# Moving bulk copies between DMA queues, and four orders of work, in a hybrid decoder-layer kernel

## The chip, the cores and the metric

The kernel runs on one NeuronCore of one Trainium2 chip. The metric is the device time of one execution in microseconds (us), the median over several runs. TensorE is written PE, its weight loads PEld, VectorE is DVE, ScalarE is ACT, GpSimd is POOL, SyncE is SP. SP does no arithmetic here: it issues DMA transfers. ACT and POOL issue some too.

## What is computed

One decoder layer for a prompt of 512 tokens and for 8 sample sequences of 4 new tokens each (32 tokens), with shared weights of width 1024. Cut to what matters:

```python
proj = h @ w_in                                   # q, k, v, z, xBC, dt
att  = dilated attention over k, v (16 heads; the samples also over 2048 cached rows)
xbc  = silu(causal_dwconv(xBC)); dt = softplus(dt + bias)
y    = ssd_scan(xs, dt, A, B, C, D)               # chunks of 128 tokens
ssm  = gated_rmsnorm(y, z, ssm_norm_g)
h1   = layer_norm(ALPHA * h + concat(att, ssm) @ w_out)
q    = h1 @ w_q; top 16 + top 16 keys -> 16 of 16384 experts for each of 8 heads
out  = layer_norm(ALPHA * h1 + sum_k gate * gelu(h1 . u[e]) * v[e])
new_k_sample, new_v_sample = caches shifted by 4 rows, with the 4 new rows at the end
```

The last line is bulk traffic: two caches of 8 x 2048 x 1024 floats are copied from HBM to HBM, less four rows each.

## The kernel before, in words

The five engines run one program each (lines 2367 to 2424 list the stages) and meet at semaphores. The stages, in order:

**Projection.** `sp_project` (L292) loads the transposed tokens `xraw` in two halves, chunks 0 to 3 and chunks 4 to 7 of the width, with the small dt weights between them, then streams 44 blocks of `w_in` through a ring of four slots. A product is made in three passes: ACT casts an operand to a high part (L318 for the tokens, L326 for weights), DVE (tokens, L377) or POOL (weights, L363) subtracts to get the low part, and PE multiplies high by high, high by low and low by high (`product`, L186 to L190). The first product is the dt projection, whose chunk c waits for the tokens' low part and for dt's low part, made after chunk 3 (L380). ACT also issues part of the cache copies here: `copy_cache` (L272, issue L277) moves 4088 KB, `copy_half` (L279, issue L283) 2044 KB. `copy_half(eng, y)` for y from 0 to 31 is all of the second cache.

**Attention.** A loop of 67 rounds n, over 64 units (16 heads x 4 tiles of 128 queries), written out by hand. In round n PE makes the scores of unit n (L666), turns the probabilities of unit n - 2 (L673) and multiplies those of unit n - 3 with the values (L682). DVE adds the bias (L785), finds the maximum (L788) and scales (L795); ACT takes the exponential (L860) and copies the turned tile out of the bank (L868). The eight sample sequences b are laid over it: sequence b begins at round 2 + 7b and `at` counts rounds from there (`sample_steps`, L587). At `at` 0 and 1 PE makes its scores from a ring of keys, at 5 and 6 it turns the probabilities, which ACT keeps (L884, L886, L887), at 7 and 9 it multiplies with a ring of four blocks of cached values (L732): blocks 0 to 3 at `at` 7, blocks 4 to 6 at `at` 9. SP loads the block four ahead into a slot as soon as its block is used (`values_of`, L610). At `at` 10 DVE copies the result (L828), at `at` 11 PE turns it (`dec_turn_out`, L736, matmul L741), as the first thing after the round's scores and before `turn(n - 2)`. After its last load SP issues the copies y = 15 to 18.

**SSD.** PE turns and sums five tiles ("fronts", L1064 to L1078), then runs four chunks of 128 tokens and the sample tile. A chunk is `state` (L1118), four `intra` (L1106), four `seg` (L1089 to L1092, two of them for the next chunk) and `inter` (L1130). At the end of chunk i, for i from 1, PE turns the normed chunk i - 1 (`turn_out`, L1031, transpose L1035), which DVE makes late in chunk i (`normed`, L1314, statement L1323); ACT copies it to `mixT` (`keep_out`, L1160, copy L1161). DVE's whole part begins with a wait for the norm vector `normg` (L1245). SP loads it at the start of the stage (L984), then two states, then issues six `copy_cache` and one `copy_half`; after the last chunk's state it stores that and streams `w_out`, with four more `copy_half` (y = 11 to 14) between its first blocks (`sp_out`, L1430). The event orders at L935 to L950 hold each engine's order; each wait asks for a count in such an order.

**Output projection.** 16 chunks of `mixT` by 16 blocks of `w_out` in a ring of eight (L1480), for tiles 0 and 1, then 2, then 3; then the first layer norm.

**Query.** 16 blocks of `peer_wq` by the tokens. SP loads blocks into four raw slots, and issues y = 19 to 31 of the second cache between them (`sp_query`, L1619). ACT, for block f, waits for the query product of f, keeps it (L1707), and casts the raw block f + 4 as soon as it has landed (`hi_of`, L1630, cast L1633). POOL makes the low part (L1640) and so frees the raw slot. PE makes the product of f + 1, then the scores of f (L1689), which need what ACT kept.

**Up and value stages.** 128 blocks of `peer_u` and then 128 of `peer_v` in the same three-pass way, with the choice of experts, the gathers and the gates on DVE and POOL beside them, then the second layer norm. The change touches nothing here.

## Time and profile before

| what | us |
|---|---|
| median of 3 runs | 2127.38 |
| the runs | 2119.74, 2127.38, 2133.82 |
| the profiled execution | 2123.87 |
| its span, first to last instruction | 2122.0 |
| PE busy | 2027.4 (96%) |
| DVE busy | 1488.1 (70%) |
| ACT busy | 743.7 (35%) |
| POOL busy | 784.4 (37%) |
| DMA moved | 683.04 MB |

All stage times below are us from the start of that span. A busy PE is not a PE at full rate, since ends of matmuls are modelled and the clock can be granted at half; so the granted clock is read with it. "Idle before, and what ended it" is inferred from semaphores. The stages lie at: projection 0 to 291, attention 291 to 518, SSD to 640, output projection to 794, query to about 926, up stage to 1560, value stage to 2084.

### The profile page before, as it was taken

To read this page: it belongs to the slowest core of one execution; us is meant where nothing else is said; L and a number is where in the kernel's file an instruction comes from. 1 tells how busy PE (TensorE), PEld (TensorE's weight loads), DVE (VectorE), ACT (ScalarE), POOL (GpSimd) and SP (SyncE) were. 2 spreads that over 40 slices of the span, in tenths; PEclk is the share of its full clock that TensorE was granted. 3 is DMA by queue.
4 is the path that set the end of the run, shared out by engine and by line. 5 is a ranking of instruction groups with operands and counts; after the bars stand their busy time and mean duration, and the time that the engine had idled before them with its cause. 6 is when DMAs were issued, how large, how long until landed. Compare 5 with 4: busy or idle time off the path is not lost.

```text
span 2122.0 us, 33482 instructions
## 1 busy us (share of the span) xinstructions
PE 2027.4 (96%) x12142; PEld 1687.3 (80%) x12142; DVE 1488.1 (70%) x3108; ACT 743.7 (35%) x1112; POOL 784.4 (37%) x483
## 2 busy tenths in 40 slices
PE   7999999997989999899999999999989999999998
PEld 7999965554553339899999999999978887777776
DVE  1276135553672335579889699999689898888988
ACT  3232124443440012134343355655333333333332
POOL 4333310000210003248899732122456555555530
PEclk9999999998989999999999999999999999999999
DMA  8999988788998479738999888878999999999993
GB/s 320 343 331 321 314 316 336 307 324 280 321 335 309 163 290 334 288 123 291 353 354 359 285 308 305 305 277 297 395 384 390 392 392 390 390 383 388 382 363 138
DMA packets 202350, 683.04 MB, mean 322 GB/s; under 512 B 18304, under 2 KB 84224, under 8 KB 194176
## 3 DMA queue, kind: packets, MB, share of 16 engines
q1 hardware_dynamic: 150256, 442.42, 58.0%
q0 software_dynamic: 46080, 167.79, 20.7%
q10 hardware_dynamic: 5904, 71.39, 9.8%
q8 instruction: 65, 1.06, 0.2%
q14 instruction: 45, 0.37, 0.0%
HBM read 618.78 MB, written 196.32 MB: 384 GB/s over the span
## 4 chain that ended last, share of the span: by engine, by line
PE 51%; DMA 24%; issue 11%; DVE 7%; POOL 4%; ACT 2%; SPq 0%; POOLq 0%; DVEq 0%; ACTq 0%
DMA overlay<-peer_v 17%; PE bank L188 10%; PE bank L189 9%; PE bank L190 9%; PE bank L1480 5%; PE bank L2082 4%; POOL overlay L363 4%; DVE overlay L2294 2%; PE bank L682 2%; DMA overlay<-peer_wq 2%; PE bank L666 2%; DMA arena<-w_out 1%; DMA overlay<-peer_u 1%; DVE arena L2095 1%; PE bank L732 1%
## 5 line engine op out<-in xcount | busy, mean ns | idle before, releaser
L188 PE MATMUL bank<-overlay 128*128 128x384 f32 (+4 forms) x2768 | 941.5, 340 | 40.3 <-DVE overlay L2300 21.1
L189 PE MATMUL bank<-overlay 128*128 128x384 f32 (+4 forms) x2768 | 926.5, 335 | 0.0
L190 PE MATMUL bank<-overlay 128*128 128x384 f32 (+4 forms) x2768 | 926.2, 335 | 0.0
L188 PEld LDWEIGHTS bank<-overlay 128*128 128x128 f32 (+1 forms) x2768 | 521.3, 188 | 88.5 <-issue 36.4
L190 PEld LDWEIGHTS bank<-overlay 128*128 128x128 f32 (+1 forms) x2768 | 520.6, 188 | 31.5
L189 PEld LDWEIGHTS bank<-overlay 128*128 128x128 f32 (+1 forms) x2768 | 521.4, 188 | 30.3
L1919 POOL DMA_INDIRECT arena<-peer_v,arena x160 | 263.2, 1645 | 223.6 <-DVE arena L2095 206.3
L1640 POOL TENSOR_TENSOR overlay<-overlay 128x1024 fp32r<-128x1024 f32 x86 | 206.6, 2404 | 293.2 <-ACT overlay L1633 289.5
L1633 ACT CAST overlay<-overlay 128x1024 fp32r<-128x1024 f32 x144 | 150.1, 1044 | 160.3 <-DMA overlay<-peer_u 88.2
L2095 DVE SCALAR_TENSOR_TENSOR arena<-arena 128x1024 f32<-128x1024 f32 x160 | 204.9, 1281 | 0.1
L1919 POOL DMA_INDIRECT arena<-peer_rows,arena x80 | 107.3, 1341 | 246.8 <-DVE arena L2090 227.0
L2294 DVE TENSOR_TENSOR overlay<-overlay 128x1024 fp32r<-128x1024 f32 x128 | 156.3, 1221 | 42.8 <-ACT overlay L2202 42.8
L2202 ACT CAST overlay<-overlay 128x1024 fp32r<-128x1024 f32 x128 | 134.4, 1050 | 142.8 <-DMA overlay<-peer_v 140.7
L363 POOL TENSOR_TENSOR overlay<-overlay 128x1024 fp32r<-128x1024 f32 x44 | 106.1, 2422 | 173.0 <-ACT overlay L326 173.0
L1992 ACT ACTIVATE arena<-bank 128x384 f32<-128x384 f32 x128 | 63.9, 499 | 206.5 <-PE bank L190 201.0
L2206 ACT CAST overlay<-overlay 128x384 fp32r<-128x384 f32 x128 | 65.6, 513 | 198.1 <-DVE overlay L2290 198.1
L1480 PE MATMUL bank<-arena 128*128 128x512 f32 x256 | 116.5, 606 | 1.3 <-DMA arena<-w_out 1.3
L2031 ACT COPY arena<-bank 128x512 f32<-128x512 f32 x96 | 104.0, 1135 | 36.0 <-PE bank L2082 36.0
L1780 DVE SCALAR_TENSOR_TENSOR arena<-arena,bank 128x1024 f32<-128x1024 f32 x80 | 96.3, 1213 | 23.0 <-DMA arena<-peer_rows,arena 22.8
L2126 DVE TENSOR_SCALAR arena<-arena 128x128 f32<-128x128 f32 x384 | 106.7, 354 | 0.0
L2082 PE MATMUL bank<-arena 128*128 128x128 f32 x768 | 101.1, 274 | 0.0
L2082 PEld LDWEIGHTS bank<-arena 128*128 128x128 f32 x768 | 99.1, 191 | 0.0
(241 smaller groups left out, 2131.7 us busy)
## 6 DMA issues: line engine op xcount, KB each, us to landing
overlay<-peer_u SPq DMA_DIRECT2D x128, 512.0 KB, 7.2
overlay<-peer_v SPq DMA_DIRECT2D x128, 512.0 KB, 11.5
o_vsall<-cache_vall SPq DMA_DIRECT2D x22, 2044.0 KB, 28.0
o_ks<-cache_k ACTq DMA_DIRECT2D x10, 4088.0 KB, 17.8
arena<-cache_kT SPq DMA_DIRECT2D x32, 896.0 KB, 11.0
arena<-cache_v SPq DMA_DIRECT2D x56, 512.0 KB, 6.5
arena<-w_out SPq DMA_DIRECT2D x48, 512.0 KB, 5.7
act<-arena SPq DMA_DIRECT2D x128, 192.0 KB, 7.8
```

Source lines behind the costliest of these rows:

```text
L188: pe.matmul(out, lhs[0], rhs[0], start=start, stop=False)
L189: pe.matmul(out, lhs[0], rhs[1], start=False, stop=False)
L190: return pe.matmul(out, lhs[1], rhs[0], start=False, stop=stop)
L363: pool.tensor_tensor(ws[1][:, s], wraw[:, s], ws[0][:, s].bitcast(F32), ALU.subtract).then_inc(w_lo, 1)
L1480: mm = pe.matmul(bank[:, 2 * (i % 2) + half, :], mixT[:, c, i * P:(i + 1) * P], w[:, half * 512:(half + 1) * 512], start=(c == 0), stop=(c ...
L1633: act.copy(us[0][:, s], uraw[s]).then_inc(u_hi, 1)
L1640: pool.tensor_tensor(us[1][:, s], uraw[s], us[0][:, s].bitcast(F32), ALU.subtract).then_inc(u_lo, 1)
L1919: pool.indirect_dma_start(gring[g % RING], None, table, bass.IndirectOffsetOnAxis(ap=at, axis=0)).then_inc(row_in[g % RING], 16)
L2082: mm = pe.matmul(bank[:, 4 + w % 4, j * P:(j + 1) * P], hot_b[:, w % 2, j], hot_a[:, w % 2, j], start=True, stop=True)
L2095: dve.scalar_tensor_tensor(acc, gring[r], w[:, bass.ds(j, 1)], acc, ALU.mult, ALU.add).then_inc(row_done, 1)
L2202: act.copy(vs[0][:, j], vraw[:, k]).then_inc(v_hi, 1)
L2294: dve.tensor_tensor(vs[1][:, j], vraw[:, k], vs[0][:, j].bitcast(F32), ALU.subtract).then_inc(v_lo, 1)
```

## The change

It has five parts. (1) The tokens come in four pieces of two chunks, the dt weights ahead of them, and ACT and DVE split dt first. (2) `dec_turn_out` moves from before `turn(n - 2)` to the end of its round. (3) The copies y = 15 to 18 are issued by ACT at the head of rounds 47, 51, 55 and 59 and not by SP after its last load; the copies 19 to 31 are issued by ACT, one after each of the first 13 `hi_of`, and not by SP between the loads of `peer_wq`. (4) In SSD, PE turns the normed chunk i - 1 not at the end of chunk i but in chunk i + 1 after `state`, for the last one after `intra(QT, 0)`. (5) DVE waits for `normg` not at the start but in `normed(0)`, before its first use.

```diff
--- before.py
+++ after.py
@@ -242,7 +242,7 @@
         consts_in, dtw_in = sem("consts_in"), sem("dtw_in")
-        x_in = [sem(f"x_in{s}") for s in range(2)]
+        x_in = [sem(f"x_in{s}") for s in range(4)]
         x_hi, x_lo = sem("x_hi"), sem("x_lo")
@@ -290,9 +290,9 @@
         def sp_project(sp):
-            sp.dma_start(xraw[:, 0:4], t["xT"][:, 0:4]).then_inc(x_in[0], 16)
             sp.dma_start(dtw_raw, t["w_dt"]).then_inc(dtw_in, 16)
-            sp.dma_start(xraw[:, 4:8], t["xT"][:, 4:8]).then_inc(x_in[1], 16)
+            for k in range(4):
+                sp.dma_start(xraw[:, 2 * k:2 * k + 2], t["xT"][:, 2 * k:2 * k + 2]).then_inc(x_in[k], 16)
             sp.dma_start(oldconv, t["state_conv"]).then_inc(consts_in, 16)
@@ -313,12 +313,11 @@
         def act_project(act):
+            act.wait_ge(dtw_in, 16)
+            act.copy(dtw[0], dtw_raw).then_inc(x_hi, 1)
             for c in range(DC):
-                act.wait_ge(x_in[c // 4], 16)
+                act.wait_ge(x_in[c // 2], 16)
                 act.copy(xs[0][:, c], xraw[:, c]).then_inc(x_hi, 1)
-                if c == 3:
-                    act.wait_ge(dtw_in, 16)
-                    act.copy(dtw[0], dtw_raw).then_inc(x_hi, 1)
@@ -364,20 +363,19 @@
                 lo(0, s)
-            pool.wait_ge(x_in[0], 16)
-            pool.wait_ge(x_in[1], 16)
+            for k in range(4):
+                pool.wait_ge(x_in[k], 16)
             pool.tensor_copy(xsam, xraw[:, :, SEQ:]).then_inc(sam_in, 1)
...
         def dve_split_x(dve):
+            dve.wait_ge(x_hi, 1)
+            dve.tensor_tensor(dtw[1], dtw_raw, dtw[0].bitcast(F32), ALU.subtract).then_inc(x_lo, 1)
             for c in range(DC):
-                dve.wait_ge(x_hi, c + 1 + c // 4)
+                dve.wait_ge(x_hi, c + 2)
                 dve.tensor_tensor(xs[1][:, c], xraw[:, c], xs[0][:, c].bitcast(F32), ALU.subtract).then_inc(x_lo, 1)
-                if c == 3:
-                    dve.wait_ge(x_hi, 5)
-                    dve.tensor_tensor(dtw[1], dtw_raw, dtw[0].bitcast(F32), ALU.subtract).then_inc(x_lo, 1)
@@ -385,7 +383,7 @@
             for c in range(DC):
-                pe.wait_ge(x_lo, 5 if c < 4 else c + 2)
+                pe.wait_ge(x_lo, c + 2)
                 for half in range(2):
@@ -640,8 +638,6 @@
                             values_of(KB * b + kb + 4)
-            for y in range(15, 19):
-                copy_half(sp, y)
@@ -759,8 +755,6 @@
                         dec_scores(b, 2 * at + 1)
-                    if at == EVERY + 4:
-                        dec_turn_out(b)
                 if 2 <= n < UNITS + 2:
@@ -772,6 +766,9 @@
                     values(n - 3)
+                for b, at in sample_steps(n):
+                    if at == EVERY + 4:
+                        dec_turn_out(b)
@@ -889,6 +886,8 @@
             for n in range(ROUNDS):
+                if n in (47, 51, 55, 59):
+                    copy_half(act, 15 + (n - 47) // 4)
                 for b, at in sample_steps(n):
@@ -934,8 +933,8 @@
         pe_ssd = Events(sem("pe_ssd"), fronts("x_turned sums") + order((0, "seg0 seg1")) +
-            chunks((0, 0, "state y0 seg2 inter y1 seg3 y2"), (1, 0, "seg0"), (0, 0, "y3"), (1, 0, "seg1"), (0, 1, "out_turned")) +
-            order((QT, "y0 seg2 y1 seg3 y2 y3 out_turned " + by_seq("state") + " last_turned")))
+            chunks((0, 0, "state"), (-1, 1, "out_turned"), (0, 0, "y0 seg2 inter y1 seg3 y2"), (1, 0, "seg0"), (0, 0, "y3"), (1, 0, "seg1")) +
+            order((QT, "y0"), (QT - 1, "out_turned"), (QT, "seg2 y1 seg3 y2 y3 out_turned " + by_seq("state") + " last_turned")))
         act_ssd = Events(sem("act_ssd"), fronts("x_kept b_kept cb_kept eacs etot wexp") + order((0, "E0 E1")) +
@@ -1134,8 +1133,14 @@
             seg(0, 1)
+            def turn_normed(i):
+                dve_ssd.wait(pe, i, "t_inter")
+                pe_ssd.count_done(i, "out_turned", turn_out(pe, i - 1, 0))
+
             for i in range(QT):
                 state(i)
+                if i >= 2:
+                    turn_normed(i - 1)
                 intra(i, 0)
@@ -1145,10 +1150,8 @@
                 seg(i + 1, 1)
-                if i:
-                    dve_ssd.wait(pe, i, "t_inter")
-                    pe_ssd.count_done(i, "out_turned", turn_out(pe, i - 1, 0))
             intra(QT, 0)
+            turn_normed(QT - 1)
             seg(QT, 2)
@@ -1242,7 +1245,6 @@
         def dve_ssd_run(dve):
-            dve.wait_ge(normg_in, 16)
             dve.wait_ge(consts_in, 96)
@@ -1316,6 +1318,8 @@
                 dve_ssd.wait(dve, i, "rstd")
+                if i == 0:
+                    dve.wait_ge(normg_in, 16)
                 if i:
@@ -1620,10 +1624,8 @@
                 sp.dma_start(uraw[s], t["peer_wq"][s]).then_inc(u_in[s], 16)
-            copy_half(sp, 19)
             with sp.Fori(1, QF // 4) as k:
                 for s in range(4):
-                    copy_half(sp, k * 4 + (16 + s))
                     sp.wait_ge(u_lo, k * 4 + (s - 3))
@@ -1699,13 +1701,17 @@
             act.sem_inc(q_kept, 2)
-            with act.Fori(0, QF // 4) as k:
-                for s in range(4):
-                    f = k * 4 + s
-                    act.wait_ge(q_ready, f + 1)
-                    act.wait_ge(s_ready, f + 1)
-                    act.copy(qT[:, s % 2].rearrange("p (h n) -> p h n", h=2), bank[:, 2 * (s % 2):2 * (s % 2) + 2, 0:HALF]).then_inc(q_kept, 1)
-                    hi_of(act, s, k + 1)
+            def query(k, s):
+                f = k * 4 + s
+                act.wait_ge(q_ready, f + 1)
+                act.wait_ge(s_ready, f + 1)
+                act.copy(qT[:, s % 2].rearrange("p (h n) -> p h n", h=2), bank[:, 2 * (s % 2):2 * (s % 2) + 2, 0:HALF]).then_inc(q_kept, 1)
+                hi_of(act, s, k + 1)
+
+            for f in range(QF):
+                query(f // 4, f % 4)
+                if f < 13:
+                    copy_half(act, 19 + f)
             for g in range(1, FOLD):
```

## Rows read from the trace of the kernel before

**Rows 1.** The page: busy time by engine, and DMA share in 40 slices

```profile
PE 2027.4 (96%) x12142; PEld 1687.3 (80%) x12142; DVE 1488.1 (70%) x3108; ACT 743.7 (35%) x1112; POOL 784.4 (37%) x483
...
DMA  8999988788998479738999888878999999999993
```

**Rows 2.** Waits of PE, whole span: us in total, times, longest us

```profile
PE bank L188 <- DVE overlay L380: 11.4, 1, 11.4
PE bank L1064 <- DVE arena L1254: 8.6, 1, 8.6
PE bank L1689 <- ACT arena L1707: 8.1, 1, 8.1
PE bank L1035 <- DVE arena L1323: 7.7, 3, 3.3
```

**Rows 3.** Windows: length; PE, PEld, DVE, ACT, POOL busy (count); clock, DMA share, GB/s

```profile
450.00:455.00 5.00, 5.00 (x52) 2.76 (x50) 3.09 (x7) 1.44 (x4) 0.00 (x0) 1.00 1.03 423
465.00:470.00 5.00, 5.00 (x54) 2.90 (x57) 3.40 (x8) 2.08 (x7) 0.00 (x0) 1.00 0.08 28
...
865.00:870.00 5.00, 5.00 (x29) 4.39 (x29) 2.58 (x12) 0.00 (x0) 1.46 (x1) 0.68 0.91 325
```

**Rows 4.** Timeline of the start: start, length, engine, line, operation [idle before]

```profile
11.42 0.41 PE L188 MATMUL bank<-overlay 128*16 128x272 f32 x1 [11.42 <-DVE overlay L380]
...
14.49 9.48 POOL L363 TENSOR_TENSOR overlay<-overlay 128x1024 fp32r<-128x1024 f32 x4 [13.44 <-ACT overlay L326]
```

**Rows 5.** Timeline of attention round 13, DVE and PE

```profile
340.16 0.49 DVE L795 TENSOR_SCALAR arena<-arena 128x512 f32<-128x512 f32 x1
...
340.56 0.42 DVE L828 COPY arena<-bank 128x256 f32<-128x256 f32 x1
...
341.04 0.71 PE L741 MATMUL bank<-arena 128*128 128x128 f32 x4 [1.31 <-DVE arena L828]
```

**Rows 6.** DMA queues in 30 to 40 us: packets, MB, share of 16 engines

```profile
q10 hardware_dynamic: 157, 2.58, 75.0%
q1 hardware_dynamic: 164, 0.61, 18.8%
```

**Rows 7.** Attention, rounds 46 to 60: a DMA issue group (453 to 466), and the timeline

```profile
arena<-cache_v SPq DMA_DIRECT2D x2, 512.0 KB, 12.8
...
453.60 0.24 ACT L868 COPY arena<-bank 128x128 f32<-128x128 f32 x1
...
467.40 0.25 ACT L887 COPY arena<-bank 32x128 f32<-32x128 f32 x1
...
469.77 1.93 PE L732 MATMUL bank<-arena 128*32 128x256 f32 x32
...
492.19 0.24 ACT L868 COPY arena<-bank 128x128 f32<-128x128 f32 x1
...
499.65 2.09 PE L732 MATMUL bank<-arena 128*32 128x256 f32 x16 [1.47 <-DMA arena<-cache_v]
```

**Rows 8.** Landing times of all w_in loads (source L300)

```profile
DMA to landing us min/median/max: 3.6/17.6/30.1
```

**Rows 9.** SSD: two pieces of the chain (start, length), and the timeline

```profile
517.90 11.35 DMA arena<-ssm_norm_g
...
609.01 31.26 DMA arena<-w_out
...
577.64 2.20 DVE L1323 SCALAR_TENSOR_TENSOR arena<-arena 128x512 f32<-128x512 f32 x2
...
579.99 1.07 PE L1035 MATMUL bank<-arena 128*128 128x128 f32 x8 [2.21 <-DVE arena L1323]
```

**Rows 10.** Query: ACT keeping products of blocks 1, 2 and 8

```profile
810.50 0.61 ACT L1707 COPY arena<-bank 128x544 f32<-128x544 f32 x1 [1.44 <-PE bank L190]
...
817.97 0.61 ACT L1707 COPY arena<-bank 128x544 f32<-128x544 f32 x1 [1.07 <-PE bank L190]
...
873.95 0.61 ACT L1707 COPY arena<-bank 128x544 f32<-128x544 f32 x1 [1.88 <-PE bank L190]
```

## The prediction, made before the result was known

> **What bounds the kernel now.** I read the page first: PE is busy for 2027 of 2122 us, and the DMA engines are at 0.8 to 1.0 in most slices, so two resources are nearly full at once [rows 1]. Then the list of what PE waited for [rows 2], since an edit of order can only give back PE's idle time and the slow clock behind it. Four entries lie at the places that change. The windows then show two things [rows 3]: after an idle stretch PE works at a clock between the two levels, 2.4 and 1.2 GHz (0.68 of full in 865 to 870, behind the 8 us hole), and DMA has a gap at 465 to 470 (8% busy). Last I read, place by place, the timeline, the chain and the DMA queues.
>
> **The change, part by part.** The sum is made against the profiled execution, 2123.87 us (span 2122.0, 1.87 around it); the median of the three runs, 2127.38, is 3.5 above it and the runs spread over 14.
>
> (1) *Start.* PE's first matmul is at 11.42, behind dt's low part, which waits for four token casts [rows 4]. Dt first and pieces of half the size let PE start some 3 or 4 us sooner. But the next product needs the low part of the first weights. POOL makes four of them in 9.48 us from 14.49, 2.37 each: the first is there at 16.9, behind all eight token casts on ACT, and the last tokens land no earlier since the bytes are the same. Dt's product now runs to 17.8 by the same timeline, so at most 0.9 us is left, or 1.2 if ACT's casts end a little sooner. PE may also sit idle at 14 to 16.5 and start slower. SP issues three more transfers ahead of the weights, 0.4 us each. Between -1 and +1.5; I take +1.
>
> (2) *Samples turned later.* Four times PE waits about 1.3 us for DVE's L828; one such place is shown [rows 5]. In round 13 the next thing on PE, `turn(n - 2)`, needs L795, which ends at 340.65, while L828 starts at 340.56 and PE goes at 341.04. Without the turn in front PE could go some 0.3 us sooner, not 1.3: the wait is handed to `scaled`. Four times 0.3 is +1.2 us; all four gaps would be 5.
>
> (3a) *Copies 15 to 18 in attention.* They go to ACT's queue, which runs beside SP's and not behind it. The projection shows how two busy queues share: in 30 to 40 us q10 (ACT's) moved 157 packets and q1 (SP's) 164, one for one, though a copy packet has 16 KB (2.58 MB by 157) and a load packet 4 KB [rows 6]. Together that is 3.19 MB in 10 us, so a copy of 2.09 MB costs 6.5 us of all 16 engines, and 128 load packets that run beside one need (128 / 15.7) 8.2 us. The Trainium skill ("DMA: Bandwidth & Descriptors", Queues, rings and completion order) says that each engine takes turns between queues by packets; the trace agrees (157 to 164).
> Where do they fall? ACT reaches round 47 at 453.6 (the last thing of round 46 is L868 there), round 51 at 467.4 and round 59 at 492.2 [rows 7]. SP's loads of cached values issued at 453 land 12.8 us later, at 466 [rows 7], for a use at 470.8 (the third of the four blocks that PE starts on at 469.77, 0.48 each) [rows 7]. Copy 15 puts 6.5 us before that: 472.6, already 1.8 late. Copy 16, issued at 467.4, runs into the tail and can add 6.5 more: 8.3 late. I take 6.8, as the tail has over 128 packets left when it starts. In round 60 PE waited 1.47 for a block that landed at 499.6 [rows 7], with the old copies behind it in the same queue. Three blocks (1.57 MB), moved from 493 at the 423 GB/s of a stretch with loads alone [rows 3], are through at 496.8; beside copy 18 at 503.3, so 3.7 later than now, I take 4. Copy 17 falls in an idle stretch. A hole of 8 us is followed by 5 us at a clock of 0.68, 1.6 us [rows 2, 3]; I add one, since around 500 the clock is low today. ACT also issues four transfers of some 0.6 us ahead of its work; 0.5. Sum of 3a: -(6.8 + 4 + 1.6 + 0.5) = -12.9 us. Its bounds are 0 (the loads have slack after all) and -18.
>
> (4, 5) *SSD.* Today `normg`, queued behind 8.4 MB of copies, lands 11.35 us after its issue at 517.90 [rows 9], and DVE, told to wait for it first, holds PE for 8.6 [rows 2]. Both the copies and the early wait go. On PE that frees 8.6 and about 2 of slow clock. The turn after `state` and not before frees less than the 7.7 of rows 2. In chunk 1 PE is through its last `seg` at 577.8, DVE's L1323 is through at 579.84 and PE goes at 579.99 [rows 9]; with `state` first (1.7 us, 580.89 to 582.61 in the same timeline) the turn still waits 0.5 us, and the next `intra` is 1.7 earlier. Twice 1.7 is 3.4. For the last chunk it gives nothing, since `intra(QT, 0)` needs a mask that DVE makes after the same L1323. PE's path is shorter by 14.
> But DMA is full from here to 640, and the third block of `w_out` lands at 640.27, and the chain of what ended last runs through it [rows 9]. This queue is one line: everything behind `normg` is unchanged. It starts sooner only by what `normg` gains: an undisturbed load of 512 KB takes 3.6 us [rows 8], so 521.5 and not 529.25: 7.7 us. So the third block lands 7.7 earlier, PE arrives 14 earlier, and a new wait of 5 to 6 us on `w_out` takes the rest, with a slow clock behind it (2.2). Gain +5.5; bounds +3 and, if the queue drains faster, +14.
>
> (3b) *Query.* A block's load now stands behind a copy in one queue. The cadence of PE is 7.46 us a block (810.50 to 817.97), so ACT should keep block 8 at 810.50 + 7 x 7.45 = 862.65; it does at 873.95 [rows 10]: 11.3 us lost, the 8.1 of rows 2 and 3.2 of slow clock. In the changed kernel loads and copies alternate, so a load is served in 8.2 us [rows 6] whatever the backlog of copies, and blocks 4 to 7 are loaded before any copy has been issued. The first contended one, block 8, is issued when POOL has freed its slot, one block after ACT kept block 0, and is cast after block 4 is kept: three cadences or 22 us later. The drift is 8.2 - 7.45 = 0.75 us a block, over 8 blocks 6 us, inside that slack. ACT then has per block 0.6 of keeping, 1.05 of cast and 0.6 of issue in 7.45. The copies end later, around 910, next to the first loads of `peer_u`; I take 0.8 for that. Gain +10.5; bounds 0 and +11.3.
> The skill's page named above has a section (Issuing engines are not separate DMA queues) that speaks against this part: issuing on several engines "will only save the time on the sequencer". By that rule 3b and 3a would both be 0, and the sum 2116. Rows 6 say that the bytes per us are shared but the order is not, and the order is what 3b lives on.
>
> What follows the query keeps its length: PE is full in the up stage and DMA at 0.9 in the value stage [rows 1], and every transfer there starts by what comes before.
>
> Sum: +1 + 1.2 - 12.9 + 5.5 + 10.5 = 5.3 us gained. 2123.87 - 5.3 = 2118.6; I say 2119.
>
> **The rivals.** A measurement of this kernel can tell about 1% (21 us) from no change.
> *A, attention is not hurt.* If copies 15 and 16 find the gap at 465 to 470 [rows 3], and loads have more slack than the 4.7 us between 466 and 470.8, 3a costs 1 and the sum is 17.2: 2107. For: DMA is at 0.81 over attention. Against: the values are loaded just in time, as round 60 shows.
> *B, the w_out line moves with PE as well.* If the four copies between the first blocks of `w_out` are not what they wait for, SSD gives its full 14; with A that is 25.7: 2098; with the forecast's attention 2110. Against: the 31.26 us that one block needs [rows 9].
> *C, slower: query loads starve.* If a copy takes more than its packet's turn on the slowest of the 16 engines, a load needs over 10 us. From 7.45 + (22 + 6) / 8 = 10.95 us on (22 of slack, and 6 that PE works on the next product meanwhile) PE waits again, at the same place, L1707; at 12.4 us a block it waits 8 x 1.45 = 11.6, and the query gains nothing. With 3a at -18 and SSD at +3: 1 + 1.2 - 18 + 3 = -12.8: 2137. The sign turns where 3a and 3b together lose more than the other 7.7. For: landings of 30 us [rows 8]. Against: in the projection the same sharing cost PE almost nothing.
> *D, the queue makes no difference.* A load still shares the same 16 engines with the copies, lands as late as now and costs PE the same 11.3 us in the query, and attention loses nothing: 1 + 1.2 + 5.5 = 7.7: 2116. It is told from the forecast by the trace, not by the time. (It is what the skill's section would give.) Against: rows 6.
>
> **How the numbers follow.** The forecast (attention loses about what the query gains), 2119, has 0.50, own range 2111 to 2127; A 0.24; B 0.10, mostly in its faster form; C 0.06; D 0.10. Faster by over 1% needs 2106 or less: most of B, a third of A and a tail of the forecast, 0.20. Slower by over 1% needs 2149: 0.03, the tail of C. Within 1%: 0.77. The range reaches down to 2102, between A and the fast form of B, and up to 2132, past the forecast without the query's gain (2129).
>
> **What would show each step right or wrong.** Start: PE's L188 wait on L380 falls from 11.4 to 7 or 8, the second product starts at 16.5. Attention: a wait of PE L732 on `cache_v` of 4 to 8 us near 471 and one of 4 to 6 near 505; without them A is right. L741's waits go, L673's grow. SSD: L1064's wait is gone, L1035's total is under 2 plus the last chunk's 3.3, and L1480 waits 5 to 6 us on `w_out`. Query: L1689's wait on L1707 is gone and the landing of `peer_wq` loads falls under 18 us; if that wait is 8 us or more, C is right. The forecast is wrong if the time is under 2111 or over 2127.

## The result, and the profile after

| what | before | after |
|---|---|---|
| median of 20 runs each, us | 2118.41 | 2128.19 |
| the runs | 2108.53 to 2133.82 | 2119.85 to 2142.40 |
| ratio, 95% interval | | 1.0045 [1.0025, 1.0065] |
| span of the profiled execution | 2122.0 | 2125.8 |
| granted clock over the span | 0.984 | 0.981 |

The changed kernel is slower by 0.45%, about 10 us, where 5 us gained had been forecast. Of the 15 us between the two, 5.5 belong to the base of the sum and to none of its terms: the profiled execution of before, against which the sum was made, took 2123.87 us and lies 5.5 above the median that 20 runs give. By the spans of the two profiled executions the loss is 3.8 us.

The waits of PE come first (us in total, times, longest), of the changed kernel:

```profile
PE bank L188 <- DVE overlay L2306: 18.8, 15, 5.7
PE bank L1484 <- DMA arena<-w_out: 13.1, 2, 7.6
PE bank L728 <- DMA arena<-cache_v: 12.4, 3, 6.2
PE bank L669 <- DVE arena L792: 9.3, 12, 2.4
PE bank L188 <- DVE overlay L378: 8.3, 1, 8.3
PE bank L1105 <- DVE arena L1275: 4.0, 2, 3.5
...
PE bank L1034 <- DVE arena L1327: 0.7, 2, 0.4
PE bank L1063 <- DVE arena L1256: 0.7, 1, 0.7
```

Of the four entries of [rows 2] that the change aimed at, three are gone or small, `normg` (8.6 to 0.7), the kept query product (8.1 to nothing) and the normed chunks (7.7 to 0.7, with 4.0 now at the last chunk's mask, L1275), and one is shorter, dt's low part (11.4 to 8.3). In their place stand two waits for DMA, 12.4 us on cached values and 13.1 us on `w_out`. What the new order of work gave back of PE's waits, waits for transfers took again.

The stages, from the first instructions that mark them in both traces (us from the start of the span):

| stage | before | after | gained | forecast |
|---|---|---|---|---|
| start and projection, to attention's first matmul | 297.8 | 296.4 | +1.4 | +1 |
| attention, to the first front of SSD | 219.3 | 236.0 | -16.7 | -12.9 + 1.2 |
| SSD and output projection, to the last `w_out` matmul | 274.4 | 274.6 | -0.2 | +5.5 |
| query, to the first gelu | 140.2 | 130.4 | +9.8 | +10.5 |
| up and value stages, to the end | 1190.3 | 1188.4 | +1.9 | 0 |

Two of the five miss by about 5 us each, attention and SSD. This table sets one execution against one, and a stage's length differs between executions of the same code. The kernels of the experiments give further draws, since most share all but one or two stages, code and queued transfers, with one of these two. They come from several chips, on which the kernel before took 2115.9 to 2127.8 us. Lengths in us:

| stage | as in the kernel before | as in the changed kernel |
|---|---|---|
| start and projection | 297.8, 299.6, 300.1, 301.9, 302.3 | 293.4, 293.6, 296.4, 298.1, 298.2, 300.9, 301.2 |
| attention | 215.2, 219.3, 222.9 | 236.0 |
| SSD and output projection | 274.4, 278.6, 281.1 | 265.4, 270.4, 274.6 |
| query | 133.2, 135.5, 140.2, 143.1 | 130.4, 130.4, 130.4, 130.4, 130.6 |

So the loss in attention is far outside the scatter. The -0.2 of SSD sets the shortest of three against the longest of three, the 9.8 of the query is one draw of something between 3 and 13, and the 1.4 of the start is inside its scatter. The places, in the timeline of PE in the changed kernel (start, length, instruction, idle time before it and what ended it):

```profile
474.57 2.07 PE L728 MATMUL bank<-arena 128*32 128x256 f32 x16 [5.71 <-DMA arena<-cache_v]
510.18 3.20 PE L728 MATMUL bank<-arena 128*32 128x256 f32 x24 [6.18 <-DMA arena<-cache_v]
637.62 8.66 PE L1484 MATMUL bank<-arena 128*128 128x512 f32 x16 [7.57 <-DMA arena<-w_out]
652.72 6.21 PE L1484 MATMUL bank<-arena 128*128 128x512 f32 x8 [5.57 <-DMA arena<-w_out]
```

The first two are where they were foretold, behind the copies that ACT issued at 452.05 and 463.72 and behind the one of 497.96. How the two queues shared in attention, by the DMA queues of the changed kernel in 456 to 462 (packets, MB, share of 16 engines):

```profile
q10 hardware_dynamic: 117, 1.91, 74.7%
q1 hardware_dynamic: 112, 0.72, 29.1%
```

One for one, as in [rows 6]. And the windows around the two holes, changed kernel (length; PE, PEld, DVE, ACT, POOL busy; clock, DMA share, GB/s):

```profile
470.00:475.00 5.00, 0.43 (x5) 0.20 (x8) 0.00 (x0) 0.00 (x0) 0.00 (x0) 0.51 1.00 419
475.00:480.00 5.00, 5.00 (x57) 2.19 (x53) 1.13 (x4) 0.49 (x2) 0.00 (x0) 0.50 0.96 347
...
505.00:510.00 5.00, 0.00 (x0) 0.00 (x0) 0.00 (x0) 0.04 (x1) 0.00 (x0) 0.76 0.74 304
510.00:515.00 5.00, 4.79 (x30) 1.81 (x30) 0.00 (x0) 0.00 (x0) 0.00 (x0) 0.50 0.01 6
515.00:520.00 5.00, 5.00 (x15) 2.54 (x13) 1.82 (x6) 1.07 (x3) 0.00 (x0) 0.50 0.00 0
520.00:525.00 5.00, 5.00 (x15) 3.00 (x14) 1.24 (x4) 0.86 (x3) 0.00 (x0) 0.50 0.00 0
525.00:530.00 5.00, 4.21 (x16) 2.51 (x15) 2.80 (x8) 1.96 (x5) 0.00 (x0) 0.50 0.00 0
```

Two things stand in them. After the second hole PE works at the lower of its two levels (0.50 of 2.4 GHz is 1.2) for four windows, 20 us. And the DMA engines, full from here on in the kernel before, do nothing for some 20 us: the copies that filled this stretch have moved ahead, and SP issues the next only when SSD begins, at 533. The same stretch before:

```profile
500.00:505.00 5.00, 5.00 (x27) 2.22 (x20) 0.97 (x4) 0.12 (x1) 0.00 (x0) 0.50 1.02 356
505.00:510.00 5.00, 5.00 (x23) 3.06 (x23) 2.10 (x6) 1.81 (x6) 0.00 (x0) 0.86 1.01 324
510.00:515.00 5.00, 3.67 (x19) 2.43 (x19) 2.80 (x8) 2.42 (x6) 0.00 (x0) 0.82 0.95 278
515.00:520.00 5.00, 5.00 (x40) 4.83 (x39) 0.00 (x0) 2.34 (x7) 2.08 (x3) 0.84 0.96 314
```

There the clock was 0.50 for one window only.

Attention as a whole, from its first matmul to the first front of SSD, before and after, with the same 1884 matmuls on PE:

```profile
297.80:517.10 219.30, 203.45 (x1884) 117.40 (x1884) 122.20 (x336) 90.97 (x249) 0.02 (x1) 0.96 0.83 316
```

```profile
296.40:532.40 236.00, 209.14 (x1884) 118.38 (x1884) 122.17 (x336) 90.86 (x249) 0.00 (x0) 0.93 0.77 303
```

Of the 16.7 us lost, 11.0 are idle time of PE (15.9 to 26.9) and 5.7 are the same matmuls taking longer, at a mean clock of 0.93 and not 0.96.

### The profile page after: what moved, and what is told of

It is laid out like the page before. It is cut to its first block, busy times and chain, and to the rows that moved or that the text cites. A ratio compares the mean times of both kernels' runs of the same rounds, so it can differ in the third digit from the quotient of the medians.

```text
span 2125.8 us, 33417 instructions
## 1 busy us (share of the span) xinstructions
PE 2031.6 (96%) x12142; PEld 1683.6 (79%) x12142; DVE 1488.9 (70%) x3108; ACT 743.4 (35%) x1112; POOL 779.7 (37%) x483
## 4 chain that ended last, share of the span: by engine, by line
PE 54%; DMA 24%; issue 10%; DVE 6%; POOL 4%; ACT 2%; SPq 0%; POOLq 0%; ACTq 0%; DVEq 0%
DMA overlay<-peer_v 17%; PE bank L188 11%; PE bank L189 11%; PE bank L190 11%; PE bank L1484 5%; PE bank L2088 4%; POOL overlay L362 4%; DMA arena<-w_out 2%; DVE overlay L2300 2%; DMA arena<-cache_v 2%; PE bank L678 2%; PE bank L662 2%; DMA overlay<-peer_u 1%; PE bank L728 1%; ACT overlay L2208 1%
## 5 line engine op out<-in xcount | busy, mean ns | idle before, releaser
L1925 POOL DMA_INDIRECT arena<-peer_v,arena x160 | 255.4, 1597 | 229.8 <-DVE arena L2101 214.6
L1642 POOL TENSOR_TENSOR overlay<-overlay 128x1024 fp32r<-128x1024 f32 x86 | 206.8, 2406 | 298.1 <-ACT overlay L1635 294.4
L1484 PE MATMUL bank<-arena 128*128 128x512 f32 x256 | 118.9, 616 | 13.1 <-DMA arena<-w_out 13.1
L2037 ACT COPY arena<-bank 128x512 f32<-128x512 f32 x96 | 103.8, 1133 | 37.9 <-PE bank L2088 37.9
L1484 PEld LDWEIGHTS bank<-arena 128*128 128x128 f32 x256 | 48.5, 196 | 78.1 <-issue 70.9
L782 DVE SCALAR_TENSOR_TENSOR arena<-bank,arena 128x128 f32<-128x128 f32 (+1 forms) x64 | 31.4, 490 | 103.7 <-PE bank L662 92.7
```

What stands on the lines that cost most here:

```text
L1484: mm = pe.matmul(bank[:, 2 * (i % 2) + half, :], mixT[:, c, i * P:(i + 1) * P], w[:, half * 512:(half + 1) * 512], start=(c == 0), stop=(c ...
L1642: pool.tensor_tensor(us[1][:, s], uraw[s], us[0][:, s].bitcast(F32), ALU.subtract).then_inc(u_lo, 1)
L1925: pool.indirect_dma_start(gring[g % RING], None, table, bass.IndirectOffsetOnAxis(ap=at, axis=0)).then_inc(row_in[g % RING], 16)
```

## The experiments

Ten kernels were run. T is the theory throughout: a copy costs the loads that it takes turns with, one packet of a load for one of the copy, and those behind it in its queue; SSD is bounded by the transfers up to the third block of `w_out`; the order of copies and loads is what the query gains by. Each run has its own rivals, told in the text on record. Where two rows are compared, both intervals count, each 4 to 7 us wide to either side.

| run | ratio to before | 95% interval |
|---|---|---|
| changed, 3a undone | 0.9945 | [0.9913, 0.9977] |
| before + 3a | 1.0065 | [1.0031, 1.0099] |
| before + 3b | 0.9948 | [0.9917, 0.9978] |
| before + 4 and 5 | 0.9989 | [0.9958, 1.0020] |
| before + 2 | 1.0009 | [0.9990, 1.0029] |
| changed, copies 15 to 18 in 4 KB pieces | 1.0395 | [1.0365, 1.0425] |
| changed, copies 15 to 18 at rounds 60 to 63 | 0.9981 | [0.9954, 1.0008] |
| changed, copies 15 to 18 after attention | 0.9940 | [0.9914, 0.9966] |
| the same, 11 to 14 behind later `w_out` blocks | 0.9909 | [0.9886, 0.9931] |
| the same, 11 to 14 and 18 in the up stage | 0.9934 | [0.9909, 0.9958] |

**Undo 3a.** Copies 15 to 18 are SP's again, the other four parts stay.

```diff
-                if n in (47, 51, 55, 59):
-                    copy_half(act, 15 + (n - 47) // 4)
...
+            for y in range(15, 19):
+                copy_half(sp, y)
```

> The changed kernel with part 3a undone: the copies 15 to 18 are again issued by SP after its last load of attention. Theory T (the loss sits in attention, where a copy in ACT's queue holds up loads in SP's, and each stall brings some 5 to 15 us of half clock): attention is 15 to 17 us shorter than in the changed kernel, no wait on cached values over 2 us; the third block of w_out lands about 122 us after attention's end as in the kernel before (not 120), so nothing is lost or gained there; the query keeps its gain of 10. In all 10 to 12 us faster than the kernel before, ratio 0.9945 to 0.9955. Rival R (the loss sits behind attention, in the new order of SSD and its wait on w_out): attention's end moves by under 5 us, and the ratio stays over 1.000.

Attention took 214.6 us (301.2 to 515.8) and not 236.0, 0.4 us of waiting on `cache_v` was left, and the ratio to before went from 1.0045 to 0.9945: 3a costs the changed kernel about 1%, 21 us by the ratios and 21.4 in attention, more than the 15 to 17 of the text. The third block of `w_out` landed 124.3 us after the issue of `normg` (about 122 was said). Rival R is out. What PE then waited for at `w_out`, in its list of waits:

```profile
PE bank L1484 <- DMA arena<-w_out: 18.2, 3, 9.9
```

**3a alone**, the same edit the other way round on the kernel before.

> The kernel before with part 3a alone. T: 15 to 17 us slower in attention (waits of PE on cached values of 6 us in round 51 and 6 in round 60); behind it nothing is gained although the norm vector lands 3.6 us after its issue and not 11.4, as w_out comes no sooner. Ratio 1.007 to 1.008. R: within 5 us of the kernel before, 0.998 to 1.002.

Slower by 0.65%, so the sign of 3a holds by itself, at 14 us. Attention is 237.8 us long, 18.5 more than before; then SSD up to the first `w_out` matmul takes 102.2 us and not 112.3. `normg` lands in 3.5 us, since the copies ahead of it are gone, and DVE holds PE for 1.7 us and not 8.6. The text had said that nothing would be gained behind attention because `w_out` comes no sooner. That fell: the third block landed 114.7 us after the issue of `normg`, and before 122.4. Of this kernel's waits:

```profile
PE bank L730 <- DMA arena<-cache_v: 10.8, 4, 5.1
...
PE bank L671 <- DVE arena L793: 4.0, 7, 1.3
PE bank L1480 <- DMA arena<-w_out: 3.3, 2, 2.4
```

So here 3a gives back some 10 us in SSD of what it costs in attention. In the changed kernel it seems to give back less: SSD up to the first `w_out` matmul is 105.2 us with 3a and 105.7 without. But the kernel with 4 KB pieces below has the same SSD and took 101.7, so that the difference is not clear of the scatter.

**3b alone**: ACT issues the copies 19 to 31 in the query, as in the diff of the change.

> The kernel before with part 3b alone (copies 19 to 31 on ACT's queue in the query). T: the 8 us wait of PE's scores on ACT in the query and the slow clock behind it go, 9 to 11 us, ratio 0.995 to 0.996. Rival (the end of the copies collides with the up stage and gives it back): under 4 us, ratio over 0.998.

Faster by 0.52%, 11 us (5 to 18 by the interval); from the last `w_out` matmul to the first gelu it took 130.4 us, as in the changed kernel, and 140.2 before. The wait that it removes is not the same in every execution. In the kernels with 3a alone and with part 2 alone, whose query is that of before, it was

```profile
PE bank L1689 <- ACT arena L1707: 1.7, 1, 1.7
```

```profile
PE bank L1690 <- ACT arena L1708: 3.6, 2, 2.5
```

and 10.5 in the run of 4 and 5. In the changed kernel the two queues moved, in 840 to 850:

```profile
q10 hardware_dynamic: 184, 2.71, 73.6%
q1 hardware_dynamic: 212, 0.79, 21.7%
```

That is 21 load packets a us beside the copies, 128 in 6.0 us, under the 7.45 of a block. The Trainium skill ("DMA: Bandwidth & Descriptors", Issuing engines are not separate DMA queues) has it that issuing on several engines only saves sequencer time; for this edit it would give no change, and the interval excludes that. The bytes per us are shared; what a load stands behind is not.

**4 and 5 alone.** SSD's event order, the late turn, and the wait for `normg` in `normed(0)`, on the kernel before.

> The kernel before with parts 4 and 5 alone (the turn of a normed chunk later, the norm vector awaited at its first use). T: PE's wait of 8.6 us at the start of SSD goes and the chunks are 3 us shorter, but the third block of w_out still lands 122 us after attention's end, so a wait of PE on w_out of 9 to 12 us takes it all: within 2 us of the kernel before, ratio 0.999 to 1.0005. Rival (w_out is not what bounds): 8 to 14 us faster, ratio 0.993 to 0.996.

No change that can be measured (0.9989). The wait for `normg` (8.6) is gone, the one for the turned chunks is 0.7 us and no longer 7.7, and PE waits for `w_out` instead, 21 us and not the 9 to 12 of the text, since the third block landed 129 us after the issue of `normg` and not 122:

```profile
PE bank L1485 <- DMA arena<-w_out: 21.3, 2, 10.9
```

PE stood at the first `w_out` matmul 15 us sooner after the start of SSD (97.6 us and not 112.3), and 20 us more of waiting on `w_out` took its place. Rival B of the prediction, the `w_out` transfers moving with PE, is out.

**2 alone.** `dec_turn_out` at the end of its round, on the kernel before.

> Before with part 2 alone: the samples' result is turned at the end of its round. Step under test: four waits of 1.3 us in front of L741 go and 0.3 us each is gained, since PE then waits for the scaled probabilities (L795) in its next turn (L673 here). The stage would be 1 us shorter, ratio 0.999 to 1.000, the waits of L741 gone and those of PE for L795 grown by about 4 us. Rival: the whole 5 us is gained (the waits of PE for L795 do not grow, ratio 0.9975). Second rival, drawn from the changed kernel, where these waits were 9.3 us and not 4.0: nothing is gained or some us are lost.

1.0009 with an interval across 1, and the wait went where it was said to: L741's 5.1 us in four are gone, and

```profile
PE bank L673 <- DVE arena L796: 8.5, 11, 1.5
```

stands where the run of 3a alone, without part 2, has 4.0. By the waits, 0.6 of 5.1 us is gained; neither the stage (218.7 us) nor the time can show so little. The first rival is out, the second is not told apart. Round 13 of the changed kernel shows it, PE's next turn waiting for the scaled probabilities and not for the copy:

```profile
341.05 0.49 DVE L792 TENSOR_SCALAR arena<-arena 128x512 f32<-128x512 f32 x1
341.45 0.42 DVE L825 COPY arena<-bank 128x256 f32<-128x256 f32 x1
...
341.60 0.66 PE L669 MATMUL bank<-arena 128*128 128x128 f32 x4 [0.98 <-DVE arena L792]
```

It waited 1.31 before [rows 5] and waits 0.98 now: 0.3 a place, as reckoned.

**Does a load wait by packets or by bytes?** The changed kernel with its four copies in attention cut in pieces of 4088 bytes and not 16352, so 512 packets a copy and not 128.

```diff
+            cutout = lambda ap, lo: ap.rearrange("b s d -> b (s d)")[:, bass.ds(y * (CHUNK // 2) + lo, CHUNK // 2)]\
+                .rearrange("b (s n) -> s b n", n=PIECE // 8)
...
-                    copy_half(act, 15 + (n - 47) // 4)
+                    copy_small(act, 15 + (n - 47) // 4)
```

> The changed kernel with the copies 15 to 18 cut into pieces of 4088 bytes (512 a copy) instead of 16352 (128), the same bytes at the same places on ACT's queue. Theory P (the two queues take turns packet by packet): beside such a copy a load gets half of the DMA engines and not a fifth, so the cached values of rounds 51 and 60 land 3 to 5 us sooner, PE's waits on them fall from 12.4 us in all to 3 to 7, and the ratio to the kernel before falls to 0.999 to 1.002 (it was 1.0045). Rival Q (the queues share by bytes, or the loads are late only by the bytes moved ahead of them): the waits stay within 2 us of 12.4 and the ratio at 1.003 to 1.006.

Both theories fell. The kernel is 4% slower, and PE waited

```profile
PE bank L735 <- DMA arena<-cache_v: 70.1, 9, 21.4
```

The queues in 475 to 485 and the window of five us within, in which PE did nothing:

```profile
q1 hardware_dynamic: 181, 0.66, 51.5%
q10 hardware_dynamic: 182, 0.74, 47.0%
```

```profile
475.00:480.00 5.00, 0.00 (x0) 0.00 (x0) 0.00 (x0) 0.00 (x0) 0.00 (x0) 0.50 1.07 167
```

The queues still take turns one for one. But the engines moved 36 packets a us here, against 32 in [rows 6] and 38 in 456 to 462 of the changed kernel, whose copy packets are four times as large. A load packet and a copy packet together took as long as before, so the small pieces do not shorten a load's turn (128 packets in 7.1 us, 6.9 in the changed kernel), and the copy keeps taking turns for 512 / 18.2 = 28 us and not 8 or less. Both theories had let this time shrink with the size of the copy's packet. By the shares the copy packet itself did get cheaper (47.0% of 160 us in 182 packets is 0.41 us each, and 0.76 in [rows 6]), but the load packet beside it dearer (0.46 and not 0.18); why is not shown.

**The copies behind attention, but in ACT's queue.**

```diff
-                if n in (47, 51, 55, 59):
-                    copy_half(act, 15 + (n - 47) // 4)
+                if n in (60, 61, 62, 63):
+                    copy_half(act, n - 45)
```

> The changed kernel with copies 15 to 18 issued by ACT at rounds 60 to 63 and not 47 to 59: behind the last load of cached values, as before, but in ACT's queue. Theory T (a copy costs only the loads that it takes turns with): attention is as long as with part 3a undone (215 us, no wait on cache_v over 1 us), normg is no longer behind the copies in a line but beside them and lands in about 8 us and not 12.5, and w_out lands no later than with 3a undone, since the bytes ahead of it are the same: ratio to before 0.992 to 0.996. The loss of 3a is then one of its rounds and not of its queue. Rival Q: it is ACT's issuing itself, or the queue, that costs (ACT's issue instructions ahead of its exponentials): attention is 5 us or more longer than with 3a undone, ratio 0.998 or more.

Attention was 216.7 us long, so it is not ACT's issuing nor its queue that cost 3a's 18.5 and 21.4 us in attention, but the rounds. The rest of T's text missed: `normg` took 13.0 us beside the copies (12.5 behind them) and not 8, and PE waited longer for `w_out`:

```profile
PE bank L1484 <- DMA arena<-w_out: 22.5, 2, 17.5
```

The ratio, 0.9981, is one that Q had said, though Q's reason, a longer attention, is out; its interval reaches T's range too. It doesn't tell whether this kernel is worse than the one with 3a undone.

**The copies 15 to 18 after attention**: 15 to 17 behind the 13 of the query, 18 behind block 1 of the up stage, all ACT's.

```diff
-                if n in (47, 51, 55, 59):
-                    copy_half(act, 15 + (n - 47) // 4)
...
-                if f < 13:
-                    copy_half(act, 19 + f)
+                copy_half(act, 19 + f if f < 13 else f + 2)
...
+                if n == 1:
+                    copy_half(act, 18)
```

> The changed kernel with the copies 15 to 18 not in attention: ACT issues 15 to 17 behind the query's other copies, one a block, and 18 in the second block of the up stage. T: attention loses nothing (as with 3a undone), SSD's line starts with the norm vector at once and so does w_out, 7 us sooner than with 3a undone; the copies end about 26 us later than before, where DMA has room. Ratio 0.990 to 0.993. Rival (the copies hold up peer_u as they held up the cached values): PE waits on the low part of peer_u's first blocks, 0.995 or more.

Ratio 0.9940, a little above T's range, which its interval reaches; the rival's 0.995 is inside the interval too, but its wait did not come (3.7 us on `peer_u`'s low part, as in the kernel before). Attention 213.6 us, SSD to the first `w_out` matmul 97.5 (105.2 in the changed kernel), and one wait on `w_out` in place of two:

```profile
PE bank L1482 <- DMA arena<-w_out: 4.4, 1, 4.4
```

**And 11 to 14 out of the first blocks of `w_out`.**

```diff
-                if i < 2:
-                    copy_half(sp, 2 * i + 11)
-                    copy_half(sp, 2 * i + 12)
...
+                if c in (26, 30, 34, 38):
+                    copy_half(sp, 11 + (c - 26) // 4)
```

> The previous kernel with the copies 11 to 14 taken from between the first blocks of w_out and issued by SP behind its blocks 26, 30, 34 and 38. T (the first blocks of w_out are what SSD ends on, late by the bulk traffic ahead of them in the same queue): the third block lands 13 us sooner (two copies), PE's waits on w_out of 13 us fall to under 4, and the ratio to 0.985 to 0.988. Rival (the copies among the later blocks hold up w_out there, whose ring has eight slots): a wait of PE on w_out of over 5 us after 740, ratio 0.990 or more.

0.9909, the fastest ratio of all and clearly below both kernels, though above the 0.985 to 0.988 looked for, and not clear of the run before it (the intervals overlap). The third block landed 97.3 us after the issue of `normg` and not 111.4, 14 sooner (13 was said). But the copies hold up other blocks: PE's waits for `w_out` have moved from 640 to 740 and later (6.1 us in three), as the rival said, though the longest is 4.2 and not over 5.

```profile
763.09 3.53 PE L1481 MATMUL bank<-arena 128*128 128x512 f32 x4 [4.15 <-DMA arena<-w_out]
```

**And 11 to 14 into the up stage**, where DMA has its widest gap.

```diff
-                if c in (26, 30, 34, 38):
-                    copy_half(sp, 11 + (c - 26) // 4)
...
-                if n == 1:
-                    copy_half(act, 18)
+                if n in (1, 4, 7, 10, 13):
+                    copy_half(act, 18 if n == 1 else 10 + (n - 1) // 3)
```

> The changed kernel without any copy between the last loads of cached values and the first blocks of peer_wq except those that stand ahead of w_out: copies 15 to 17 behind the query's copies as in the runs before, and now 18 and 11 to 14 issued by ACT behind blocks 1, 4, 7, 10 and 13 of the up stage, where the profile before has the DMA engines at 0.32 and 0.64 (900 to 980). Theory T (each copy costs only what it pushes out of the line of loads behind it): w_out is loaded without a copy in its line, PE waits under 2 us there, and in the up stage one copy of 6.5 us for three blocks (14.7 us) is hidden by the ring of four: ratio 0.985 to 0.989, below the 0.991 of the run that kept them behind later blocks of w_out. Rival R: a block of peer_u needs 8.2 us beside a copy and PE uses one in 4.9, so that each copy holds PE by about 3 us and the slow clock follows: ratio 0.992 or more, with waits of PE for the low parts or of ACT for peer_u in the first 16 blocks.

0.9934: no better than leaving them where they were (0.9940). Rival R is right in kind. From the first gelu to the last, the stage took 630.5 us, against 624.3 in the run before and 623.8 to 625.5 in the eleven other profiles together; PE's low parts come late, since the loads do. Its size was less than R's 3 us a copy: 5 to 7 us for the five.

```profile
PE bank L188 <- POOL overlay L1637: 8.2, 4, 3.7
```

The windows of this run, in which the previous one has PE busy for all of the 20 us:

```profile
940.00:960.00 20.00, 18.41 (x105) 18.09 (x104) 17.80 (x77) 10.13 (x13) 15.68 (x8) 1.00 0.98 360
960.00:980.00 20.00, 17.45 (x100) 17.13 (x99) 11.25 (x45) 8.03 (x11) 12.64 (x9) 1.00 1.00 400
```

A gap in DMA's share is not free where the consumer takes a block every 4.9 us and a load beside a copy needs more.

## Why the prediction was wrong

**Start, part 2 and the query came out, as far as they can be told.** The wait for dt's low part is 8.3 us (7 to 8 was said) and the second product starts at 16.59 (16.5). The 1.4 us gained up to attention fit the 1 forecast, but no run had part 1 by itself, and the same start differs by 4 to 8 us between profiles, so that the agreement may be luck. Part 2 gained 0.6 by its waits where 1.2 was reckoned, and its wait went to the named instruction. The query gained 9.8 (10.5) in this pair; that the wait went is shown in every kernel with 3b, its size is that of one execution. One sign failed there: `peer_wq` loads issued in the loop still land 22.4 us after issue (median; 29.3 before) and not under 18, since SP issues several at once and they stand behind each other; their rate is what counts, and it sufficed. Rival A is out by the 12.4 us on `cache_v`, C by the query, and D by the run of 3b alone.

**Attention: the step that failed is the clock behind the stalls.** The step said 6.8 + 4 us of stall more than today. Measured: 12.4 us on `cache_v` less the 1.47 before [rows 7], 10.9, so the stalls were right. The failed term is "a hole of 8 us is followed by 5 us at a clock of 0.68, 1.6 us; I add one". The rows of the whole stage give 5.7 us in its place, by which the same matmuls took longer: PE was at 0.50 in 475 to 480 and then in the four windows from 510 to 530. With the idle time (11.0, where the terms for stalls, issuing and part 2 make 10.1) that is all of the 5.0 by which the stage missed. The run of 3a alone agrees: PE busy for 213.35 us in attention, where the nine profiles without copies in these rounds have 199.9 to 208.3. The prediction had two reasons to take more. The 0.68 is the mean of a window in which the clock changed:

```profile
861.40:868.00 6.60, 3.39 (x13) 2.79 (x14) 1.06 (x4) 1.56 (x2) 2.34 (x1) 0.50 0.93 348
868.20:870.00 1.80, 1.80 (x17) 1.80 (x16) 1.70 (x11) 0.00 (x0) 0.00 (x0) 1.00 0.99 386
```

And its own count for the query puts 3.2 us of slow clock to that same hole, where this step took 1.6 and counted only one hole of two. A us of stall cost 1.5 us here (16.7 / 11.0).

**SSD: the step missed in this pair of profiles, but the other profiles do not show it wrong.** The step is "everything behind `normg` starts 7.7 us sooner, so the third block lands 7.7 earlier". The first half is right: `normg` landed in 3.6 us and not 11.35, and the copies were through. The third block landed 122.4 us after `normg`'s issue before (517.90 to 640.27) and 119.5 after (533.21 to 652.72), 2.9 earlier and not 7.7. Those 4.8 are most of what the stage missed in this pair (5.5 forecast, -0.2 measured, 5.7), and PE waited 13.1 us for `w_out` where 5 to 6 was said. But the same time can be read in the other kernels with the same queue up to that block. Where the copies stand ahead of `normg` in SP's queue it was 122.4, 124.3, 126.5, 127.4 and 129.1 us; where they do not, 111.4, 114.7, 115.9 and 119.5. (With the copies beside it, at rounds 60 to 63, it was 129.3.) The pair of the prediction is the shortest of the five and the longest of the four. Two of the others, 3b alone (`normg` issued at 523.29, so 127.4) and the 4 KB pieces (issued at 605.48, so 115.9), in pieces of their chains:

```profile
616.79 33.88 DMA arena<-w_out
```

```profile
684.56 36.79 DMA arena<-w_out
```

The means are 10.5 us apart (125.9 and 115.4), and the groups do not overlap; on one and the same chip it was 124.3, 127.4 and 129.1 against 114.7. So the copies ahead did move `w_out`, and by more than was said; that the stage gained nothing in the pair is a matter of which executions were profiled. By the means of the profiles in the table of stages it gained 8 (278.0 to 270.1), with the forecast, 5.5, inside their scatter.

What differs between executions is how far the queue runs ahead of a block. The DMA engines in just these two stretches, before and after:

```profile
517.90:640.30 122.40, 104.12 (x447) 63.87 (x445) 74.80 (x88) 51.71 (x92) 23.68 (x24) 0.89 0.98 332
```

```profile
533.20:652.70 119.50, 100.98 (x448) 61.17 (x445) 74.83 (x88) 51.73 (x92) 25.36 (x24) 0.91 0.96 337
```

The rate is the same, and so are the bytes, 40.6 and 40.3 MB. SP issues 35.1 MB from `normg` up to and with the third block (six copies of 4.19 MB, three of 2.09, seven transfers of 0.52). So when the third block had landed in the changed kernel, some 5.2 MB of what was issued behind it had been moved as well. With 3a alone, the same queue, it was 2.8 (37.9 MB, 330 GB/s for 114.7 us). What sets this stays open.

**The parts, and what is left.** Measured alone on the kernel before, 3a costs 14 us, 3b gains 11, 4 and 5 gain 2 and part 2 loses 2 (the last two within their intervals), and about 1 is gained at the start. That sums to a loss of 2, each part with an interval of 4 to 7 us each way; the measured loss is 10, with an interval from 5 to 14. The two prices of 3a, 14 and 21, point to a loss that comes only when 3a meets 4 and 5, but their intervals overlap, and it is not shown that there is one.

Against the sum, then: 5.3 us were to be gained; the clock in attention takes 4.1 and the other terms of the stage 0.9, and the profile against which the sum was made was slow by 5.5. That leaves a loss of 5, at the near end of the interval. The rest, which this pair of profiles puts in SSD, is not assigned. The forecast's shape (attention loses about what the query gains, SSD is bounded by `w_out`) held but for the price of the slow clock.

## What to carry to other kernels

Price a copy at every queue it touches, by packets: while it runs, each packet of a load in another queue pays one packet of the copy, and here pieces of 4 KB were no cheaper for it than 16 KB. A copy belongs where the loads have slack longer than that or where no load waits, and a gap in DMA's share does not prove slack; here thirteen copies cost nothing that shows in the query, beside loads of one block per 7.45 us, five cost 5 to 7 us in the up stage and four 18 to 21 in attention. Price the slow clock behind each stall, and from rows at the place. And before a step of 5 us is called right or wrong, read the same stage in several profiles of the same code: here it differed by 8 us in attention, 7 to 9 in SSD with the output projection, and 10 in the query.

## What the runs showed that was not expected

- Beside a load queue, a copy from HBM to HBM in 4088-byte packets let no more packets through than one in 16352-byte packets: 363 packets and 1.40 MB in 10 us, against 321 and 3.19 MB in [rows 6].
- A stall of about 6 us was followed by 20 us at the lower clock level (510 to 530), one of the same length (474.57) by 5. The second came 36 us behind the first, and in the 20 us after it the DMA engines stood idle and DVE and ACT did little; what decides between 5 and 20 us was not tried.
- ACT issued copy 16 ahead of arithmetic that stands before it in the program, here by 1.2 us. The last work of round 50 ended at 464.97, and the issue, at the head of round 51, began at 463.72:

```profile
463.72 0.61 ACTq L283 DMA_DIRECT2D o_vsall<-cache_vall  x1
...
464.72 0.25 ACT L884 COPY arena<-bank 32x128 f32<-32x128 f32 x1
```

  It had been expected at 467.4 [rows 7]; the other 2.7 us are that the round itself came sooner. The first packets of copy 15, issued at 452.05, moved between 3 and 4 us later.
- When a block of `w_out` had landed, its queue, with some 30 MB ahead of the block, had moved an estimated 5.2 MB of what was issued behind it in one kernel and 2.8 in another.
